# Convolution taps by what GpSimd does, a new order of the begin, and the logarithm's table loaded at other places

## The chip, the cores and the metric

The kernel runs on one core of one Trainium2 chip. The metric is the device time of one execution in microseconds (us), the lower the better. Engines are named as the profile names them: PE (TensorE matmul) with PEld (its weight load), DVE (VectorE), ACT (ScalarE), POOL (GpSimd), SP (SyncE, which issues most DMAs).

## The reference

Two blocks of two layers each over 256 tokens of 1024 features, float32. The first block carries two streams, x and a context c, each 256 tokens. Only the first block is touched by most of the change:

```python
for l in range(2):
    sh1, sc1, g1, sh2, sc2, g2 = adaln(c, w_mod[l], b_mod[l])   # silu(c) @ w_mod, both streams
    h  = modulate(rms_norm(x,  norm1_g[l]), sh1, sc1)
    hc = modulate(rms_norm(xc, norm1_g[l]), csh1, csc1)
    # q, k (rms-normed, rotated), v, pool input, conv inputs a and b
    q, k, v, up, ca, cb = project_inputs(h, w_in[l], q_norm_g[l], k_norm_g[l])
    ...                                    # the same for hc
    attn   = diff_attn_post(diff_attention(q, k_all, v_all, lam), ...)
    pool_o = pool_mixer(up, ...)           # moving means of 2, 4, 8, 16 tokens
    conv_o = silu(layer_norm(depthwise_conv31(ca * sigmoid(cb))))
    x = x + g1 * (concat(attn, pool_o, conv_o) @ w_out[l])
    x = x + g2 * swiglu(modulate(rms_norm(x, norm2_g[l]), sh2, sc2), ...)
    ...                                    # xc likewise, in layer 0 only
```

The second block has, per layer, two kinds of attention and a gated feed-forward with a 3-tap convolution (gate is silu); of it the change touches only where ACT loads a table.

## The kernel before

All activations lie feature-major in SBUF. Weights come from HBM in pieces of 128 x 2048 floats (1 MB) into three raw buffers (`raw`, slot = piece number mod 3), issued by SP. A weight piece of a projection is split for PE: ACT copies it to a rounded part `wh` (step `split`), then DVE makes the rest `wl` = raw - wh. Activations are split the same way (`hx_hi`, `hx_lo` and so on). A product is three matmuls: hi by wh (L1329), hi by wl (L1332), lo by wh (L1334). Pieces of `w_mod` are used raw, by 4 small matmuls each (step `mod`); eight of them make a third of a layer's modulation, which ACT copies out (`modc`) and PE and DVE finish (`modend`).

Nothing is scheduled by the hardware: `plan_program` writes one list of steps, and each engine walks that list and performs its own part of each step, in this order and with waits on semaphores. A step that waits holds back all that stands behind it on its engine. `Plan.take` hands out the next weight piece; its `look` emits the splits and DMAs that buffers allow (`Plan.look`: at most 3 split pieces are held, and a `mod` piece keeps its raw buffer until its matmuls are done).

The begin: squares of c (`nsq`, ACT; POOL adds them), four `mod` pieces, the root of c's norm (`nroot`: PE sums over features with a matrix of ones, ACT does Ln and Exp), four more `mod` pieces, `modend`, c's normalised activation (`nfin`: DVE multiplies, ACT adds the shift and rounds, DVE makes the lo part, eight chunks of 256), squares of x, the gemm of part b for c, and only then (`start_x`) the root and `nfin` of x, the lambdas of the attention, and the gemm of part b for x.

`inproj1` runs over the parts b, a, p, q0, k0, v0, q1, k1, v1 and, in each, over the streams (layer 0: c and x; layer 1: x, with a second generator for c's k and v). Part a fills a list `bg` with the 31 taps x 2 halves of the depthwise convolution of its stream, each one DVE instruction (`tap`, L1741, a scalar_tensor_tensor of 128x256); `pump(n)` emits n of them. Part p starts the moving means on POOL (`pool`, 15 instructions a stream, L2015 to L2026). From q1 on, the attention of the same layer is woven between the projections (`weave`; `scores`, `exps`, `weights`, `turned`, `values`).

After c's attention: `conv_post` (its first part takes the mean, `two` the variance, Ln, Exp, scaling and silu) for c, `pc_split` of c, the same for x, then the output projection of c woven with the attention of x and the modulation pieces of layer 1.

ACT holds one table set at a time. Silu and sigmoid need others than Ln and Exp; `fn` (L1514 to L1525) calls `preload_act_table_set` (L1518) before an Ln or Exp when another set was last used, and stands behind the wait of that step. The loads of the other sets appear at L1523.

## Time and profile before

| | |
|---|---|
| time before, median of 3 runs | 1796.46 us (1794.7 to 1797.76) |
| the profiled execution's own time | 1794.97 us |
| its span, first to last instruction | 1793.1 us |
| mean granted TensorE clock | 0.977 of full |
| PE busy | 94% of the span |
| DVE, ACT, POOL busy | 59%, 49%, 11% |

The profile is one execution. A timeline row is: start in us from the span's start, duration in us, engine, line, operation, output and inputs by the program's names, shape, how many merged, and in brackets how long the engine had been idle and what ended that. In the windows, PEclk is the granted clock as a share of full speed (1.00 is 2.4 GHz, 0.50 is 1.2 GHz).

### The profile page before, as it was taken

What the parts mean: (1) busy time and instruction counts of PE and PEld (TensorE: products, weight loads), DVE (VectorE), ACT (ScalarE), POOL (GpSimd) and SP (SyncE); (2) the same over time, 40 slices, a digit from 0 to 9 for tenths busy, and PEclk for the clock granted to TensorE, in tenths of its full rate; (3) what the DMA queues carried; (4) which work ended last, traced back from release to release, by engine and by line L of the source; (5) the groups of instructions that cost most, each with busy time, mean ns of one, the idle gap of its engine ahead of it and who ended that gap; (6) DMA issues with size and microseconds to landing.
All of it is one profiled execution on the core that took longest, in us unless ns stands there. A gap on an engine that the chain in (4) does not pass through costs nothing. (4 is left out here: it accounts for less than half of the span.)

```text
span 1793.1 us, 30262 instructions
## 1 busy us (share of the span) xinstructions
PE 1685.8 (94%) x12864; PEld 1526.0 (85%) x12864; DVE 1063.0 (59%) x1472; ACT 886.3 (49%) x1192; POOL 192.7 (11%) x138
## 2 busy tenths in 40 slices
PE   5899988999999999997999999988999999889999
PEld 2777666999999999965899989757999987679999
DVE  2498657644445444986644445755776456657773
ACT  3334555544345434555544335655555366556552
POOL 1140000122003210300022100000011000000110
PEclk7899999999999999999999999999999999999999
DMA  9233646466446545363266453302555533025553
GB/s 368 94 141 136 240 165 216 184 235 252 171 165 211 185 174 182 141 238 138 99 221 201 172 174 130 132 22 86 186 184 194 177 120 134 24 95 184 184 195 119
DMA packets 45110, 299.12 MB, mean 167 GB/s; under 512 B 5216, under 2 KB 7360, under 8 KB 11696
## 3 DMA queue, kind: packets, MB, share of 16 engines
q1 hardware_dynamic: 44304, 295.65, 46.0%
q8 instruction: 102, 1.67, 0.4%
q0 software_dynamic: 240, 0.79, 0.1%
q10 hardware_dynamic: 432, 0.75, 0.1%
q14 instruction: 32, 0.26, 0.0%
HBM read 296.10 MB, written 1.06 MB: 166 GB/s over the span
## 5 line engine op out<-in xcount | busy, mean ns | idle before, releaser
L1749 DVE TENSOR_TENSOR wl<-raw,wh 128x2048 fp32r<-128x2048 f32 (+3 forms) x236 | 529.0, 2242 | 520.8 <-ACT wh L1523 470.0
L1523 ACT ACTIVATE wh<-raw 128x2048 fp32r<-128x2048 f32 (+3 forms) x236 | 436.8, 1854 | 259.4 <-PE bank L1334 158.8
L1329 PE MATMUL bank<-hx_hi,wh 128*128 128x256 f32 x1920 | 547.9, 285 | 16.3 <-ACT hx_hi L1523 9.7
L1332 PE MATMUL bank<-hx_hi,wl 128*128 128x256 f32 x1920 | 539.8, 281 | 3.3 <-DVE wl L1749 3.3
L1334 PE MATMUL bank<-hx_lo,wh 128*128 128x256 f32 x1920 | 540.4, 281 | 0.0
L1329 PEld LDWEIGHTS bank<-hx_hi,wh 128*128 128x128 f32 x1920 | 364.0, 190 | 23.9 <-issue 19.7
L1332 PEld LDWEIGHTS bank<-hx_hi,wl 128*128 128x128 f32 x1920 | 364.3, 190 | 8.8 <-DVE wl L1749 4.6
L1334 PEld LDWEIGHTS bank<-hx_lo,wh 128*128 128x128 f32 x1920 | 363.8, 189 | 0.5 <-DVE hx_lo L1741 0.2
L1332 PE MATMUL bank<-hid_hi,wl 128*128 128x256 f32 x880 | 245.4, 279 | 0.5 <-DVE wl L1749 0.5
L1334 PE MATMUL bank<-hid_lo,wh 128*128 128x256 f32 x880 | 245.4, 279 | 0.0
L1329 PE MATMUL bank<-hid_hi,wh 128*128 128x256 f32 x880 | 245.3, 279 | 0.0
L1329 PE MATMUL bank<-hc_hi,wh 128*128 128x256 f32 x752 | 218.8, 291 | 6.2 <-issue 2.7
L1332 PE MATMUL bank<-hc_hi,wl 128*128 128x256 f32 x752 | 215.2, 286 | 7.6 <-DVE wl L1749 7.6
L1334 PE MATMUL bank<-hc_lo,wh 128*128 128x256 f32 x752 | 214.6, 285 | 1.3 <-DVE hc_lo L1856 0.8
L1332 PEld LDWEIGHTS bank<-hid_hi,wl 128*128 128x128 f32 x880 | 165.2, 188 | 0.8 <-DVE wl L1749 0.8
L1334 PEld LDWEIGHTS bank<-hid_lo,wh 128*128 128x128 f32 x880 | 165.1, 188 | 0.0
L1329 PEld LDWEIGHTS bank<-hid_hi,wh 128*128 128x128 f32 x880 | 165.0, 187 | 0.0
L1329 PEld LDWEIGHTS bank<-hc_hi,wh 128*128 128x128 f32 x752 | 146.1, 194 | 19.5 <-issue 19.2
L1332 PEld LDWEIGHTS bank<-hc_hi,wl 128*128 128x128 f32 x752 | 146.1, 194 | 9.0 <-DVE wl L1749 8.6
L1334 PEld LDWEIGHTS bank<-hc_lo,wh 128*128 128x128 f32 x752 | 146.2, 194 | 2.0 <-DVE hc_lo L1856 0.9
L1523 ACT ACTIVATE tmp<-bank,vec 128x256 f32<-128x256 f32 (+3 forms) x188 | 105.8, 586 | 70.1 <-PE bank L1334 39.7
L2031 POOL TENSOR_TENSOR hid_lo<-tmp,hid_hi 128x512 fp32r<-128x512 f32 x33 | 91.7, 2779 | 349.7 <-ACT hid_hi L1523 349.7
(208 smaller groups left out, 1955.0 us busy)
## 6 DMA issues: line engine op xcount, KB each, us to landing
raw<-in_wts SPq DMA_DIRECT2D x258, 1024.0 KB, 4.8
raw<-in_wts SPq DMA_DIRECT2D x20, 768.0 KB, 4.0
raw<-in_wts SPq DMA_DIRECT2D x4, 576.0 KB, 3.5
tmp<-tscr SPq DMA_DIRECT2D x16, 128.0 KB, 4.3
raw<-in_wts SPq DMA_DIRECT2D x2, 640.0 KB, 3.9
xTc<-in_ctxT SPq DMA_DIRECT2D x1, 1024.0 KB, 10.8
xTx<-in_xT SPq DMA_DIRECT2D x1, 1024.0 KB, 8.6
out_x<-xTx POOLq DMA_DIRECT2D x3, 256.0 KB, 5.5
```

The lines of the kernel that those rows point to most:

```text
L1329: pe.matmul(out, hi[:, k, c:c + m], x_hi, start=first and k == 0 and o == 0, stop=False, skip_group_check=True)
L1332: pe.matmul(out, lo[:, k, c:c + m], x_hi, start=False, stop=False, skip_group_check=True)
L1334: ins = pe.matmul(out, hi[:, k, c:c + m], x_lo, start=False, stop=last and k == nk - 1, skip_group_check=True)
L1523: return act.activation(out, in_, func, bias=bias, scale=scale)
L1749: tt(M.wl[k][:, 0:ne], M.raw[f["r"]][:, 0:ne], M.wh[k][:, 0:ne].bitcast(F32), ALU.subtract).then_inc(*on.inc(f["tlo"]))
L2031: tt(lo, y.t[:, :], hi.bitcast(F32), ALU.subtract).then_inc(*on.inc(t[1]))
```

## The change

It does six things. (1) In the first eight `mod` pieces `look` is made only up to the fourth, so that the split of the first projection weight comes behind `modc` and `modend`. (2) At the begin the squares of x are emitted ahead of c's `nfin`, and x's root and `nfin` directly behind c's, ahead of the first gemm; only the lambdas stay between the first two gemms. (3) `inproj1` emits 4 taps a step while POOL computes means (part p, and q0 of the first stream), 10 in the others, instead of 9. (4) `conv_post` becomes three parts; in layer 0 the Ln and Exp of c and x come together, then the silus of both, ahead of c's `pc_split`, and the round of the weave that stood idle goes away. (5) In `attention1` the first `exps` comes ahead of the first yield. (6) A step `log_set` loads the table of Ln and Exp: at the begin, behind each sigmoid, behind the silus of the convolution, behind the last silu of each feed-forward, and behind the first silu where a norm is due in the second round.

```diff
--- before.py
+++ after.py
@@ -448,7 +448,7 @@
     mod_bank, t_mod, mod_late = {}, {}, []
 
     def mod_piece(l, cb, k):
-        f = take(("mod", l, cb, k), look=k < 7)
+        f = take(("mod", l, cb, k), look=k < (4 if (l, cb) == (0, 0) else 7))
         if k == 0:
             mod_bank[0] = banks.get()
         b = mod_bank[0]
@@ -543,9 +543,10 @@
                 mul = p.gemm_tok if part[0] == "v" else p.gemm_pair
                 bank, tk = mul(f, H[s], toks[s], done=s == streams[-1])
                 hfree[s] = [tk]
+                pooling = part == "p" or part == "q0" and s == streams[0]
                 pump(2)
                 run_pending()
-                pump(7)
+                pump(2 if pooling else 8)
                 project1(l, s, part, bank, tk)
                 yield
             if pool_at:
@@ -561,6 +562,7 @@
             t_sg = ev("sig")
             sig_of[s] = (sg, t_sg)
             step("sig", b=b, tk=tk, sg=sg, free=sg.free, t=t_sg)
+            step("log_set")
             banks.give(b, t_sg)
         elif part == "a":
             sg, t_sg = sig_of[s]
@@ -628,13 +630,18 @@
 
         def two():
             v, rs = banks.get(), tmps.get()
-            t2, t_ln, t_rs, t_n, t_x = ev("mm"), ev("ln"), ev("rs"), ev("cdev"), [ev("cact"), ev("cact")]
-            step("conv2", l=l, s=s, v=v, v_free=v.free, sq=sq, a=a, rs=rs, rs_free=rs.free, t=t2, t_ln=t_ln,
-                 t_rs=t_rs, t_n=t_n, t_x=t_x)
+            t2, t_ln, t_rs, t_n = ev("mm"), ev("ln"), ev("rs"), ev("cdev")
+            step("conv2", s=s, v=v, v_free=v.free, sq=sq, a=a, rs=rs, rs_free=rs.free, t=t2, t_ln=t_ln,
+                 t_rs=t_rs, t_n=t_n)
             tmps.give(sq, t2)
             banks.give(v, t_ln)
             tmps.give(rs, t_n)
-            conv_tok[s] = [t_x[1]]
+
+            def three():
+                t_x = [ev("cact"), ev("cact")]
+                step("conv3", l=l, s=s, t_n=t_n, t_x=t_x)
+                conv_tok[s] = [t_x[1]]
+            return three
         return two
 
     mix_of = {}
@@ -707,8 +714,8 @@
             return norm
 
         scores(0)
+        exps(0)
         yield
-        exps(0)
         scores(1)
         norms = []
         for u in range(8):
@@ -792,6 +799,8 @@
         region_free[:] = [tk]
         return nrm, t
 
+    behind = []
+
     def ffn1(l, s, toks, fill=None):
         hid_toks, late = [], []
         for i in range(11):
@@ -803,6 +812,8 @@
             sl = tmps.get()
             a = ev("silu")
             step("silu", b=bg_, tk=tg, sl=sl, free=sl.free, t=a)
+            if i == 10 or i == 0 and behind:
+                step("log_set")
             banks.give(bg_, a)
             bu, tu = p.gemm_pair(("up1", l, 2 * i + 1), H[s], toks)
             y = tmps.get()
@@ -878,16 +889,12 @@
     n["c"].root()
     mod_fill(4, (0, 1, 0))
     mod_flush()
-    toks["c"] = finish0("c")
     p.look()
     for pr in range(4):
         n["x"].add(pr, t_x["x"])
-
-    def start_x():
-        n["x"].root()
-        toks["x"] = finish0("x")
-        lambdas()
-    before_x.append(start_x)
+    for s in "cx":
+        toks[s] = finish0(s)
+    before_x.append(lambdas)
     gi = inproj1(0, "cx", toks, ["b", "a", "p", "q0", "k0", "v0", "q1", "k1", "v1"])
     for i in range(13):
         next(gi)
@@ -898,11 +905,14 @@
     finish_conv(0, "x")
     p.look()
     stage_split("c", "c")
-    two.pop(0)()
+    for three in [fn() for fn in two]:
+        three()
+    step("log_set")
     pc_split("c", "c")
     idle = lambda: None
-    weave(chain(steps(lambda: two.pop(0)()), attention1(0, "x", "x")),
-          chain(steps(idle), outproj1(0, "c", "c", BY_COLS, norm)),
+    two.clear()
+    weave(attention1(0, "x", "x"),
+          outproj1(0, "c", "c", BY_COLS, norm),
           mod_steps(1, (1, 1, 3)),
           steps(idle, idle, idle, lambda: pc_split("x", "x")))
 
@@ -916,7 +926,7 @@
     next(ox)
     finish_ffn_in("c")
     weave(ox)
-    behind = [lambda: finish_ffn_in("x")]
+    behind.append(lambda: finish_ffn_in("x"))
 
     def ffn_step(i):
         mod_fill(i % 2, (1, 2, 0))
@@ -945,7 +955,11 @@
         finish_conv(1, "x")
 
     keys, proj, piece = (lambda: next(gc)), (lambda: next(gx)), (lambda: next(out))
-    norm_half, mix_half = (lambda: two.pop(0)()), (lambda: pc_split("x", "c"))
+    def norm_half():
+        two.pop(0)()()
+        step("log_set")
+
+    mix_half = lambda: pc_split("x", "c")
     fill = ((keys, proj), (proj, keys), (proj, conv_half), (norm_half, mix_half), (piece,), (piece,))
     for fns in fill:
         for fn in fns:
@@ -1278,6 +1292,8 @@
                 (yg, tg), (yu, tu) = res
                 sg, m, t = ev("silu"), ev("gate"), (ev("hid_hi"), ev("hid_lo"))
                 step("gate2", i=i, yg=yg, tg=tg, yu=yu, tu=tu, sg=sg, m=m, free=rf, t=t)
+                if i == 10:
+                    step("log_set")
                 tmps.give(yg, m)
                 tmps.give(yu, *t)
                 hid_toks.extend([t, t])
@@ -1512,11 +1528,14 @@
     eps = M.vcol("eps")
     table = [None]
 
+    def log_set():
+        if table[0] != LOG_SET:
+            act.preload_act_table_set(LOG_SET)
+        table[0] = LOG_SET
+
     def fn(out, in_, func, scale=1.0, bias=0.0, accum=None):
         if func in (ACT.Ln, ACT.Exp):
-            if table[0] != LOG_SET:
-                act.preload_act_table_set(LOG_SET)
-            table[0] = LOG_SET
+            log_set()
         elif func not in (ACT.Copy, ACT.Identity, ACT.Square):
             table[0] = func
         if accum is None:
@@ -1535,6 +1554,7 @@
         act.dma_start(M.vec[:, :], io["vecs"]).then_inc(*on.inc(t_vec, 16))
         on.wait_ge(t_c, z)
         fn(M.csil[:, :, 0:2], M.craw[:, :, :], ACT.Silu).then_inc(*on.inc(t_cs))
+        log_set()
         on.wait_ge(t_vec)
 
     def split(f, free):
@@ -1596,9 +1616,11 @@
         on.wait_ge(t_d, sq_free)
         fn(sq.t[:, :], M.pc[s][:, 2:4, :].rearrange("p a t -> p (a t)"), ACT.Square).then_inc(*on.inc(a))
 
-    def conv2(l, s, v, rs, rs_free, t, t_ln, t_rs, t_n, t_x, **_):
+    def conv2(v, rs, rs_free, t, t_ln, t_rs, **_):
         on.wait_ge(t, rs_free)
         rsqrt(rs, v.t[:, 0:T], T, 1.0 / 256, t_ln, t_rs)
+
+    def conv3(l, s, t_n, t_x):
         on.wait_ge(t_n)
         for j in range(2):
             y = M.pc[s][:, 2 + j, :]
...
```

## Rows read from the trace of the kernel before

**Rows 1.** The page of the kernel before, part 1: busy time, share of the span, instructions.
```profile
PE 1685.8 (94%) x12864; PEld 1526.0 (85%) x12864; DVE 1063.0 (59%) x1472; ACT 886.3 (49%) x1192; POOL 192.7 (11%) x138
```
**Rows 2.** Waits of PE: line, who ended the wait, us in total, times, longest.
```profile
PE bank L1332 <- DVE wl L1749: 11.4, 10, 3.7
```
**Rows 3.** Timeline of PE, 9 to 67 us: start, us, operation, [idle before <-releaser].
```profile
29.17 1.94 PE L1354 MATMUL bank<-raw,csil 128*32 128x512 f32 x8 [3.29 <-DMA raw<-in_wts]
34.05 1.12 PE L1379 MATMUL bank<-cst,tmp 128*128 128x128 f32 x4 [2.94 <-ACT tmp L1523]
...
49.48 4.11 PE L1354 MATMUL bank<-tmp,cst 128*128 128x256 f32 x10 [3.58 <-POOL tmp L2010]
...
56.95 0.58 PE L1329 MATMUL bank<-hx_hi,wh 128*128 128x256 f32 x1 [3.36 <-ACT hx_hi L1523]
...
65.69 1.06 PE L1354 MATMUL bank<-raw,csil 128*32 128x512 f32 x8
```
**Rows 4.** Timeline of ACT and GpSimd, 31 to 48 us.
```profile
31.60 1.91 ACT L1523 ACTIVATE wh<-raw 128x2048 fp32r<-128x2048 f32 x1 [6.19 <-DMA raw<-in_wts]
...
42.88 1.90 ACT L1523 ACTIVATE wh<-raw 128x2048 fp32r<-128x2048 f32 x1
...
44.69 2.18 ACT L1523 ACTIVATE tmp<-xTx 128x512 f32<-128x512 f32 x4
...
45.38 2.38 POOL L2005 TENSOR_TENSOR tmp<-tmp 128x256 f32<-128x256 f32 x1 [29.59 <-ACT tmp L1523]
```
**Rows 5.** DMA issues, window 31.1 to 31.3 us: count, size, us to landing.
```profile
raw<-in_wts SPq DMA_DIRECT2D x1, 1024.0 KB, 8.4
```
**Rows 6.** Windows: us, then PE, PEld, DVE, ACT, POOL busy, PEclk, DMA share, GB/s.
```profile
56.95:65.70 8.75, 8.75 (x51) 8.59 (x51) 7.11 (x22) 4.89 (x9) 0.00 (x0) 0.64 0.00 0
66.68:72.60 5.92, 5.92 (x54) 5.92 (x51) 0.00 (x0) 1.13 (x1) 0.00 (x0) 1.00 0.79 304
...
109.13:117.30 8.17, 8.17 (x48) 8.17 (x49) 8.17 (x13) 1.92 (x1) 4.28 (x5) 0.67 0.40 136
...
237.14:244.60 7.46, 7.46 (x49) 7.34 (x48) 3.61 (x4) 2.39 (x2) 0.74 (x1) 0.76 0.00 0
...
1074.20:1079.50 5.30, 5.30 (x34) 5.30 (x35) 5.16 (x14) 3.24 (x8) 0.30 (x1) 0.73 0.01 2
```
**Rows 7.** Taps on DVE, 86.3 to 113.9 and 113.9 to 119.6 us: ns min/median/max.
```profile
L1741 DVE SCALAR_TENSOR_TENSOR pcc<-upadc,vec,pcc x23: 855/956/1525, 88.2 to 113.1; 128x256 f32<-128x256 f32 x23
...
L1741 DVE SCALAR_TENSOR_TENSOR pcc<-upadc,vec,pcc x14: 471/473/951, 113.1 to 119.3; 128x256 f32<-128x256 f32 x14
```
**Rows 8.** Timeline of DVE and PE, 105 to 110 us.
```profile
105.92 3.15 DVE L1749 TENSOR_TENSOR wl<-raw,wh 128x2048 fp32r<-128x2048 f32 x1
...
109.13 0.58 PE L1332 MATMUL bank<-hc_hi,wl 128*128 128x256 f32 x1 [3.70 <-DVE wl L1749]
```
**Rows 9.** Timeline of ACT and PE, 213 to 237 us.
```profile
233.01 1.28 ACT L1518 ACT_TABLE_LOAD   x1 [3.89 <-DVE st L1737]
...
219.91 0.39 PE L1334 MATMUL bank<-hc_lo,wh 128*128 128x256 f32 x1 [0.75 <-DVE hc_lo L1856]
...
235.14 2.07 PE L1354 MATMUL bank<-k,q1x 64*128 64x512 f32 x2 [5.11 <-ACT e L1524]
```
**Rows 10.** Timeline of ACT and PE around the norms of the later stages.
```profile
332.20 1.28 ACT L1518 ACT_TABLE_LOAD   x1 [4.15 <-PE bank L1354]
333.49 0.47 ACT L1523 ACTIVATE tmp<-bank,vec 128x256 f32<-128x256 f32 x1
...
345.16 0.39 PE L1332 MATMUL bank<-hc_hi,wl 128*128 128x256 f32 x1 [1.56 <-DVE wl L1749]
...
1074.20 0.55 PE L1329 MATMUL bank<-hx_hi,wh 128*128 128x256 f32 x1 [3.31 <-issue]
...
1243.17 0.35 PE L1329 MATMUL bank<-hx_hi,wh 128*128 128x256 f32 x1 [2.08 <-ACT hx_hi L1523]
```
**Rows 11.** Timeline of DVE in the projections of layer 1, 774 to 792 us.
```profile
781.05 2.28 DVE L1749 TENSOR_TENSOR wl<-raw,wh 128x2048 fp32r<-128x2048 f32 x1
```

More of the change, by code:

```diff
@@ L1725, in scalar_program @@
                 "hn2": hn2, "sig": sig, "pool": pool, "poolproj": poolproj, "vcopy": vcopy, "conv1": conv1,
-                "conv2": conv2, "exp1": exp1, "turn1": turn1, "val1": val1, "sub1": sub1, "pcsplit": pcsplit,
+                "conv2": conv2, "conv3": conv3, "log_set": log_set, "exp1": exp1, "turn1": turn1, "val1": val1,
+                "sub1": sub1, "pcsplit": pcsplit,
                 "stsplit": stsplit, "silu": silu, "hidsplit": hidsplit, "lambdas": lambdas, "tables": tables,
```

## The prediction

> **What bounds the kernel now.** I read the page first: PE is busy for 1685.8 of 1793.1 us [rows 1], so a change that adds no matmul can only win idle time of PE, some 107 us, and time in which PE runs at the lower of its two clock levels. The waits of PE [rows 2] show no large single cause: the costliest is 11.4 us for `wl` from DVE, in 10 waits. So each wait is read in its stage, in the timelines, and for each the question is which engine ended it and what that engine did just before. The clock is read in the windows [rows 6]: 48 matmuls of a first projection take 8.75 us at a granted clock of 0.64 and 5.92 us at 1.00. PE stood idle ahead of the slow one. A wait thus costs its length and up to some 3 us more.
>
> **The begin.** PE waits 2.94 us for `modc`, then for c's activation, multiplies for c, waits 3.58 us for POOL's sums of x, takes 4.11 us for the root, waits 3.36 us for `hx_hi` and multiplies for x until 65.7 [rows 3]. New order: the last `mod` matmul ends at 29.17 + 1.94 = 31.1 [rows 3], and `modc` no longer stands behind a split of 1.91 us [rows 4], so `modend` is done some 2 us earlier, at about 34. But ACT and DVE now make two splits ahead of c's `nfin`. The second one's piece is issued at 31.2 and lands 8.4 us later, at 39.6 [rows 5]. ACT's half of it runs to 41.5, the four squares of x (2.18 us [rows 4]) to 43.6, DVE's half (2.3 us) to 43.8. c's `nfin` starts there instead of at 36.5: that is a loss of 7 us for the first gemm. POOL's first sum waits for DVE's split, as it does now (2.38 us [rows 4]), so the sums are ready at about 46.2 and the root runs on PE to 50.4 (4.11). c's eight chunks are out at 51 (0.8 us each, as in the chunks now), x's at about 58.5. PE multiplies for c from 50.4 to 56.2 and for x to 61.9, both at 5.8 us, as its clock is up after the root. The end moves from 65.7 to 61.9: **-3.9 us**. If the clock rises one step later it is -1.5; if POOL and DVE hinder each other less, -5.5. Nothing waits on SP: its order is the same, and the slot of the piece behind is freed by a split that ends when it does now, at 36.
>
> **The pools.** While POOL works, a tap takes 956 ns in the median, after it 473 [rows 7]: the taps advance in step with POOL's instructions. 18 taps stand between one split and the next on DVE; the one at 105.92 takes 3.15 us and PE waits 3.70 us for it [rows 8] and then runs its gemm in 8.17 us at 0.67 instead of 5.92 us at 1.00 [rows 6], and the next one's start still slowly. That is 3.7 + 2.3 + 0.9 = 6.9 us. With 4 + 4 taps ahead of it the split is done at about 98, PE asks at 101. The wait goes whole: **-6.9 us**. The 15 taps come back: 10 a step for nine steps, 4 in a tenth. Two steps then hold 20 taps x 0.4 + a split 2.3 + rotations 3.4 = 13.7 us of DVE against some 14.6 us of PE (two gemms 11.7, a `mod` piece 1.1, norm matmuls 1.9). It fits, with little room; two short waits there (0.9 and 2.0 us now) each get 0.4 us and more: **+1.5**, between 0 and 6.
>
> **The convolution's end and the output projection of c.** Now ACT loads four tables here; `exps` of x's first unit waits behind the last, at 233.01, and PE waits 5.11 us for its banks [rows 9] and then takes 7.46 us for a gemm at 0.76 [rows 6]. New: two loads fewer, and `exps` ahead of the split. Against it: with the idle round gone, the next output piece is number 35 instead of 36, so `p.look()` already splits two pieces ahead of `stage_split`; c's lo part comes 2.3 us later than at 219.91 [rows 9], at 222.2, and so does the first gemm. Then Ln, Exp (2x), two silus each, the table and `pc_split` end at 227.4 on ACT and 228.6 on DVE; the maxima end at 230, the exponentials at 231.5. The first gemm ends at about 230 with a slow start, then a `mod` piece, scores, and the second gemm starts at 233.2 instead of 237.14, one `mod` piece (1.1 us) behind, and at full clock (1.5 us): 3.9 - 1.1 + 1.6, **-4.5 us**. Bounds: -6.5, and +1.5 if the late first gemm is all that stays.
>
> **The tables at the norms.** Where a root comes after silus, Ln stands behind a load of 1.28 us [rows 10]. Beside a gemm the root delays DVE's split, and PE waits for it: 1.56 us at 345 [rows 10], and likewise 1.58 at 540 and 0.70 at 725. The load goes to an idle moment of ACT, the waits shrink by at most 1.28: -1.3 - 1.3 - 0.7 = **-3.3 us** (0 if the split behind the new load becomes as late). In two places nothing covers it: PE waits 3.31 us at 1074 (and at 1438), but 2.08 us at 1243, where the same norm has no load [rows 10]. Twice 1.23: **-2.5 us**. After 3.31 us both run at a lower clock first (0.73 for 5.3 us at 1074 [rows 6]); I take that this goes in one of the two, **-1.5** (0 to -3.1). The extra silu and log loads of the feed-forwards stand in ACT's idle time (49% busy) and cost nothing while splits are a gemm ahead.
>
> A rule is weighed here. The row of the load has 1.28 us, from the end of PE's matmul on [rows 10]. The Trainium skill (ScalarE: Activation LUTs, section What ACT_TABLE_LOAD costs) says that every switch costs the load and a drain, 2.66 us in all. By it the two uncovered norms would win 5.3 us instead of 2.5, and the sum would be 2.8 us lower. The difference of the waits, 3.31 - 2.08 = 1.23, disagrees: it is the load alone.
>
> **Layer 1.** Its pool has no wait of PE now. Fewer taps are done there by the next splits' time, good for 2.4 us of DVE. But `exps` of the first unit now stands on ACT ahead of the Exp of q1's norm and of a split: ACT has to wait for DVE's maxima at about 778.8, its exponentials end at 780.4, the split's ACT half at 783.6 and DVE's at 785.9, where it now ends at 783.33 [rows 11] and PE asks for it then. 0 to 2.7, I take **+1.3**. The log load behind the silus delays the first output piece's split by its 1.28 us: **+1.3**.
>
> **Sum**, against the profiled execution's 1794.97: -3.9 - 6.9 + 1.5 - 4.5 - 3.3 - 2.5 - 1.5 + 1.3 + 1.3 = -18.5, so 1776.5. The median of the runs is 1.5 above that execution, so **1778.0**.
>
> **The rivals.**
> - The begin of x's attention gains nothing (+4.5) and the late first gemm costs 2: 1784.5. For it: two splits ahead of `stage_split`. Against: the bank wait of 5.11 us is ended by an exponential that surely comes earlier. 0.14.
> - DVE is the bound once 10 taps stand in a step: the 5.4 us of the pools are lost and the 2.7 of layer 1 paid in full: about 1785. For it: 13.7 of 14.6 us. Against: DVE idles some 2 us before nearly each split now. 0.11.
> - The change doesn't do what it says with the tables: loads come back for the next function on ACT's way, no norm gains (+7.3): 1785.3. 0.05.
> - The low-clock stretches vanish nearly all, which the shorter waits allow: 8 us more, 1770. 0.06.
> - Slower: the exponentials that stand ahead of the splits in both layers. A late split frees its raw buffer late, so the next piece lands late too. If each of the 10 projection steps that are left beside an attention loses the 2.7 us of above, it costs 27 - 1.3 us: 1803.7. It decides from 1.85 us a step. For it: ACT's queue is strict and the piece's slot is tied to it. Against: in layer 0 DVE is not awaited there, and landings lead by more than a gemm. 0.05.
> - Forecast, 0.59, its own range 1771 to 1784.
>
> **How the numbers follow.** 1778 is the forecast's. The range holds 8 in 10: from 1769 (part of the fast clock case) to 1788 (rivals at 1785 with their spread). 0.2% (3.6 us) is about what a measurement can tell from no change. Slower by more has the slower rival's 0.05 and 0.01 of others' tails, 0.06; within it lie 0.03, the far tails of the two rivals at 1785; faster by more: 0.91.
>
> **What would show it.** PE's last matmul of the first x gemm at about 62; no wait for `wl` near 101 to 107 and 0.5 us taps only few while POOL runs; the second output gemm of c at full clock, 12 us or more earlier in the span; PE's waits of 3.31 us at 2.1; 26 table loads instead of 25, none of L1518 with idle PE behind it. Wrong would be: a wait of several us for `wl` or for `tap` after the pools, or c's first gemm past 52 with x's not right behind.

## The result

| | before | after |
|---|---|---|
| median | 1797.76 us (1794.7 to 1800.54) | 1788.25 us (1787.42 to 1791.48) |
| the profiled execution | 1794.97 | 1789.45 |
| its span | 1793.1 | 1787.7 |
| mean granted clock | 0.977 | 0.978 |

The ratio of the medians is 0.9949, 95% interval 0.9936 to 0.9962: 9.5 us faster where 18.5 had been forecast. The median lies 10.3 us above the predicted 1778.0 and a quarter of a us above the range's upper end. Of these 10.3 us, 1.3 is the base (1797.76 where the forecast had 1796.46 for the kernel before) and 9.0 the change. PE's busy time is 3.1 us less than before [rows 1] with the same number of matmuls, and the others are within 2.3 us, so only idle and low-clock time of PE has moved. Page of the changed kernel, part 1:

```profile
PE 1682.7 (94%) x12864; PEld 1524.4 (85%) x12864; DVE 1061.4 (59%) x1472; ACT 888.6 (50%) x1193; POOL 192.4 (11%) x138
```

The way to read such a pair is to take marks that both traces have (the same matmul) and to write down how much earlier each comes. Beside it stands what the forecast's terms add up to there. The last column has the same shift in a second pair of profiles, one more of each kernel, taken later (see "What one profile is worth"):

| mark on PE | before | after | shift | forecast | shift, second pair |
|---|---|---|---|---|---|
| modulation piece behind the first x gemm | 65.69 | 62.30 | -3.4 | -3.9 | -2.9 |
| `modT` matmuls, beside c's attention | 180.71 | 171.41 | -9.3 | -9.3 | -8.0 |
| norm of the convolution (`conv2`) | 213.91 | 211.93 | **-2.0** | -9.3 | -3.9 |
| last three gemms of x's output projection | 299.66 | 295.12 | -4.5 | -13.8 | -9.9 |
| first gemms of layer 1 | 717.95 | 710.21 | -7.7 | -16.4 | -11.0 |
| x's output projection in layer 1 | 870.90 | 864.86 | -6.0 | -14.5 | -7.4 |
| norm at 1074 | 1074.20 | 1066.85 | -7.4 | -15.7 | -9.6 |
| last feed-forward | 1606.73 | 1595.77 | -11.0 | -18.5 | -13.4 |
| end | 1793.1 | 1787.7 | **-5.4** | -18.5 | -13.4 |

In the first pair two places hold the difference to the forecast: 7.3 us lost between 171 and 212 us, and 5.6 us in the last feed-forward. In the second pair the first place is there again, with 4.1 us, and the last is not. The rows of each follow.

**Begin and pools.** Timeline of the changed kernel, PE from 29 to 63 us, DVE and PE from 93 to 102 (start, us, operation, idle before and who ended it):

```profile
31.43 1.12 PE L1395 MATMUL bank<-cst,tmp 128*128 128x128 f32 x4 [0.70 <-ACT tmp L1542]
46.70 4.37 PE L1370 MATMUL bank<-tmp,cst 128*128 128x256 f32 x10 [14.16 <-POOL tmp L2033]
62.30 1.07 PE L1370 MATMUL bank<-raw,csil 128*32 128x512 f32 x8
...
94.77 2.73 DVE L1772 TENSOR_TENSOR wl<-raw,wh 128x2048 fp32r<-128x2048 f32 x1 [2.22 <-ACT wh L1542]
101.46 0.28 PE L1348 MATMUL bank<-hc_hi,wl 128*128 128x256 f32 x1
```

The root waits for POOL until 46.70 (46.2 was expected), x's gemm ends at about 62.4 (61.9). DVE's split ends at 97.5 (98), PE asks at 101.46 and does not wait: the 3.70 us of [rows 8] are gone.

**The 7.3 us.** Timeline of ACT and PE of the changed kernel, 202 to 205 us:

```profile
202.59 1.91 ACT L1542 ACTIVATE wh<-raw 128x2048 fp32r<-128x2048 f32 x1 [4.32 <-DMA raw<-in_wts]
204.40 0.37 ACT L1542 ACTIVATE aT<-bank 128x256 f32<-128x256 f32 x1
204.91 2.05 PE L1370 MATMUL bank<-aT,v 128*128 128x256 f32 x4 [4.59 <-ACT aT L1542]
```

Its DMA issues in the window 195.1 to 195.2 us (count, size, us from issue to landing):

```profile
raw<-in_wts SPq DMA_DIRECT2D x1, 1024.0 KB, 7.4
```

ACT stands still for 4.32 us in front of a split whose piece, issued at 195.1, lands 7.4 us later. Behind the split stands the copy `aT`, ready for ACT since PE's transposition of 198.7, and PE has nothing else to do until it comes. After that wait PE runs at its lower level: the four matmuls of `aT` take 2.05 us where the kernel before has 1.13. In the kernel before this split comes after the attention.

**Output projection of c.** Windows as in [rows 6], of the changed kernel:

```profile
205.00:228.00 23.00, 19.89 (x88) 15.49 (x88) 11.61 (x18) 14.24 (x23) 0.00 (x0) 0.72 0.20 75
229.85:235.78 5.93, 5.93 (x54) 5.79 (x56) 3.15 (x7) 3.37 (x5) 0.00 (x0) 1.00 0.79 330
```

The stage itself won: the second output gemm takes 5.93 us at 1.00 where it took 7.46 at 0.76, and starts 7.3 us earlier (the prediction's sign was 12 or more) though the stage began only 2.0 earlier. But the first window stands at 0.72; in the kernel before the 23.1 us from 213.9 on have 0.86.

**End of x's attention.** The same pattern once more, ACT and PE, 281 to 285 us:

```profile
281.47 1.91 ACT L1542 ACTIVATE wh<-raw 128x2048 fp32r<-128x2048 f32 x1 [4.09 <-DMA raw<-in_wts]
283.28 0.37 ACT L1542 ACTIVATE tmp<-bank 128x256 f32<-128x256 f32 x1
283.70 1.22 PE L1370 MATMUL bank<-tmp,cst 128*128 128x256 f32 x2 [3.05 <-ACT tmp L1542]
```

**Tables.** PE at the places of [rows 10], and behind it ACT's groups of table loads (L1533: the logarithm's set, L1542: the others; count, us busy and mean ns, idle ahead of them):

```profile
338.72 0.39 PE L1348 MATMUL bank<-hc_hi,wl 128*128 128x256 f32 x1 [0.28 <-DVE wl L1772]
532.36 0.38 PE L1348 MATMUL bank<-hx_hi,wl 128*128 128x256 f32 x1 [0.29 <-DVE wl L1772]
1066.85 0.35 PE L1345 MATMUL bank<-hx_hi,wh 128*128 128x256 f32 x1 [2.03 <-issue]
1427.72 0.35 PE L1345 MATMUL bank<-hx_hi,wh 128*128 128x256 f32 x1 [2.03 <-issue]
```

```profile
L1542 ACT ACT_TABLE_LOAD x13 | 16.7, 1283 | 2.4 <-POOL upadc L2020 2.2
L1533 ACT ACT_TABLE_LOAD x13 | 16.7, 1283 | 0.2
```

1.56, 1.58, 3.31 and 3.31 us of waits became 0.28, 0.29, 2.03 and 2.03: each lost 1.28, the load. 26 loads, as expected, and those of the logarithm's set stood with 41.4 us of idle ACT before them and now with 0.2.

**Layer 1.** ACT and PE, 772 to 776 us, and PE at the first output gemm:

```profile
772.74 1.89 ACT L1542 ACTIVATE wh<-raw 128x2048 fp32r<-128x2048 f32 x1
774.54 0.58 ACT L1542 ACTIVATE tmp<-bank 128x512 f32<-128x512 f32 x1
775.17 0.70 PE L1370 MATMUL bank<-tmp,cst 128*128 128x512 f32 x1 [2.38 <-ACT tmp L1542]
...
805.10 0.55 PE L1345 MATMUL bank<-hc_hi,wh 128*128 128x256 f32 x1 [4.13 <-issue]
```

**The 5.6 us at the end.** Both kernels keep PE busy without a gap here, at a granted clock of 1.00. A window of 40 us in the last feed-forward of the kernel before:

```profile
1640.00:1680.00 40.00, 40.00 (x355) 40.00 (x355) 30.44 (x39) 25.62 (x31) 4.77 (x4) 1.00 0.50 171
```

The same window of the changed kernel:

```profile
1640.00:1680.00 40.00, 40.00 (x342) 40.00 (x341) 29.34 (x37) 25.16 (x29) 5.22 (x4) 1.00 0.51 182
```

And PE's timeline in the kernel before where its stream changes its pace:

```profile
1611.33 0.28 PE L1329 MATMUL bank<-hx_hi,wh 128*128 128x256 f32 x1
1611.45 0.28 PE L1332 MATMUL bank<-hx_hi,wl 128*128 128x256 f32 x1
1611.57 0.31 PE L1334 MATMUL bank<-hx_lo,wh 128*128 128x256 f32 x1
1611.72 0.28 PE L1329 MATMUL bank<-hx_hi,wh 128*128 128x256 f32 x1
1611.83 0.28 PE L1332 MATMUL bank<-hx_hi,wl 128*128 128x256 f32 x1
```

355 matmuls against 342 in the same 40 us. The same instructions start either 118 ns apart or 113 (exact start to start; the rows round to 0.12 and 0.11). With one matmul of 0.31 instead of 0.28 us at 1611.6 the one gave way to the other, and the new pace held for 77 us. Of the last feed-forward's 1584 matmuls 1110 ran at 113 in the profile of before, none in that of after: 1110 x 4.5 ns = 5.0 of the 5.6 us. So the profile from which the forecast counted was a lucky one there, and this may be why its 1794.97 stands 2.8 us under the median of 1797.76.

### The profile page after: what moved, and what is told of

Same layout as the page of the kernel before. It is cut to its first block and busy times, and to the rows that moved or that the text cites. A ratio compares the mean times of both kernels' runs of the same rounds, so it can differ in the third digit from the quotient of the medians.

```text
span 1787.7 us, 30261 instructions
## 1 busy us (share of the span) xinstructions
PE 1682.7 (94%) x12864; PEld 1524.4 (85%) x12864; DVE 1061.4 (59%) x1472; ACT 888.6 (50%) x1193; POOL 192.4 (11%) x138
## 5 line engine op out<-in xcount | busy, mean ns | idle before, releaser
L1542 ACT ACTIVATE wh<-raw 128x2048 fp32r<-128x2048 f32 (+3 forms) x236 | 437.1, 1855 | 252.7 <-PE bank L1350 158.0
L1542 ACT ACTIVATE tmp<-bank,vec 128x256 f32<-128x256 f32 (+3 forms) x188 | 105.7, 586 | 105.5 <-PE bank L1350 56.6
L1370 PE MATMUL bank<-tmp,cst 128*128 128x256 f32 (+3 forms) x294 | 113.2, 509 | 27.9 <-POOL tmp L2033 14.2
## 6 DMA issues: line engine op xcount, KB each, us to landing
xTc<-in_ctxT SPq DMA_DIRECT2D x1, 1024.0 KB, 10.7
```

The lines of the kernel that those rows point to most:

```text
L1370: return pe.matmul(out, lhsT, rhs, start=start, stop=stop, skip_group_check=True)
L1542: return act.activation(out, in_, func, bias=bias, scale=scale)
```

## The experiments

All times are medians; those of the kernel before on the same chip lay between 1797.4 and 1799.2 us. A gain in us is worked out from the ratio to them. By their 95% intervals these gains are uncertain by 2 to 4 us.

**One part alone.** Three kernels that add one part each to the kernel before. The taps:

```diff
+                pooling = part == "p" or part == "q0" and s == streams[0]
                 pump(2)
                 run_pending()
-                pump(7)
+                pump(2 if pooling else 8)
```

> The kernel before with only the taps changed (4 a step while GpSimd works, 10 in the others). The forecast's terms: -6.9 for the wait of 3.70 us near 109 and its low clock, +1.5 for the steps with 10 taps: -5.4, 1792.4 us where the kernel before has 1797.8. From the trace of the changed kernel (shift of 6.8 us over the pools, none given back up to 196 us): 1791. Rival (DVE is the bound with 10 taps a step): no gain left, 1796 to 1798, with new waits of PE for wl between 120 and 200 us.

1792.68 us, ratio 0.9958 (0.9943 to 0.9973): 7.6 us faster. The wait near 109 is gone, and PE has no wait for `wl` between 120 and 200 us: the rival falls. Both the forecast's -5.4 and a gain of 6.9 with nothing given back lie inside the interval.

The order of the begin (parts 1 and 2 of the change, as in the diff ahead):

> The kernel before with only the new order of the begin. The changed kernel's first x gemm ended 3.4 us earlier (62.4 instead of 65.8). Theory: that carries through to the end, 1794.4 us against 1797.8. Rival (the shift is absorbed at the wait for wl near 109 us, whose chain hangs on the taps and GpSimd and not on the gemms): PE's wait there grows from 3.7 to about 7 us and the total stays within 1 us of 1797.8.

1796.22 us, ratio 0.9984 (0.9969 to 1.0000): 2.9 us faster, a gain at the edge of what can be told. The row of PE at the taps' split, with the old taps:

```profile
105.30 0.58 PE L1328 MATMUL bank<-hc_hi,wl 128*128 128x256 f32 x1 [3.80 <-DVE wl L1745]
```

It waits 3.80 us, not 7, and stands 43.5 us behind the modulation piece that follows the first x gemm, as it did before (43.4): the chain of POOL and its taps moved along with the gemms. The rival falls. But its 3.8 us against [rows 8] are not all a gain of the edit: in the profiles of e4 and e5 below, which have the old begin, the same matmul comes at 106.40 and 106.20. The modulation piece behind the first x gemm starts at 62.59 to 65.69 us in the five profiles with the old begin (mean 64.2) and at 60.00 to 62.31 in the nine with the new one (mean 61.7): 2.5 us, near the 2.9 of the medians.

The tables (part 6 alone, with the step behind each `conv2`):

```diff
             step("sig", b=b, tk=tk, sg=sg, free=sg.free, t=t_sg)
+            step("log_set")
...
+            if i == 10 or i == 0 and behind:
+                step("log_set")
```

> The kernel before with only the loads of the logarithm's table at the new places. The forecast: -3.3 beside gemms, -2.5 at the two uncovered norms, -1.5 of low clock, +1.3 ahead of layer 1's first output split: -6.0, 1791.8 us against 1797.8. Rival (in the changed kernel the layer's shift between 307 and 1595 us comes from the long runs of matmuls that go at 113 or at 118 ns each, and not from the tables): 1795 or more, with the waits shorter all the same.

1791.67 us, ratio 0.9953 (0.9935 to 0.9972): 8.5 us faster, more than the forecast's 6.0, which lies inside the interval. The rival's 1795 does not.

**The part that lost.** The kernel before with parts 4 and 5, the convolution's end without the idle round and the exponentials ahead of the yield:

```diff
-    two.pop(0)()
+    for three in [fn() for fn in two]:
+        three()
     pc_split("c", "c")
...
-    weave(chain(steps(lambda: two.pop(0)()), attention1(0, "x", "x")),
-          chain(steps(idle), outproj1(0, "c", "c", BY_COLS, norm)),
+    weave(attention1(0, "x", "x"),
+          outproj1(0, "c", "c", BY_COLS, norm),
...
         scores(0)
+        exps(0)
         yield
-        exps(0)
```

> The kernel before with only the third part of the convolution's end, without the idle round, and with the first exponentials ahead of the first yield in both layers; no taps, begin or tables. The forecast had -4.5 and +1.3 for this: 3.2 us faster than before. Theory now: it also moves the first output piece one place up in the order of pieces, so that its split waits on ACT for its landing ahead of c's last attention steps (about +7), wins some 7 at the output projection, loses 3 to 4 at the end of x's attention and 2 to 4 in layer 1: 0 to 5 us slower than before. Rival (the early split hurts only because PE comes earlier in the full change): no wait of PE for aT over 2 us near 213 us, and 3 us faster than before.

1803.63 us against 1797.52, ratio 1.0027 (1.0014 to 1.0041): about 5 us **slower** (2.5 to 7.4). ACT and PE at c's last attention steps, and PE in layer 1:

```profile
207.37 1.91 ACT L1530 ACTIVATE wh<-raw 128x2048 fp32r<-128x2048 f32 x1 [3.74 <-DMA raw<-in_wts]
209.69 0.77 PE L1361 MATMUL bank<-aT,v 128*128 128x256 f32 x1 [4.67 <-ACT aT L1530]
...
783.29 1.22 PE L1361 MATMUL bank<-tmp,cst 128*128 128x512 f32 x1 [3.25 <-ACT tmp L1530]
```

The early split makes its wait without the earlier PE of the full change, so the rival falls. Layer 1 from its first gemms to its output projection takes 138.9 us here, 134.4 and 134.6 in two profiles of the kernel before. By the marks, against the mean of those two profiles, this kernel loses 5.2 us from `modT` to `conv2`, wins 5.4 from there to the last gemms of x's output projection, and loses 4.4 in layer 1.

**The split moved back.** The changed kernel with one look fewer:

```diff
-        f = take(("mod", l, cb, k), look=k < (4 if (l, cb) == (0, 0) else 7))
+        f = take(("mod", l, cb, k), look=k < (4 if (l, cb) == (0, 0) else 6 if (l, cb) == (0, 2) else 7))
```

> The changed kernel with one edit: the look at the seventh modulation piece of layer 0's last third is left out, so that the first split of an output weight comes behind c's attention instead of ahead of its last two steps. In the changed kernel this split stands on ACT at 202.59 us after 4.32 us of waiting for its piece, the last copy of the transposed scores stands behind it, and PE idles 4.59 us at 204.91 and runs at its lower clock after that. Theory (the early split is what cost the missing 7.5 us of the forecast): c's attention ends about 7 us earlier, the two splits then stand ahead of c's lo part and take some 2 to 4 us of that back; about 1783 us (1781 to 1785) where the changed kernel has 1788.3. Rival (the pieces land late anyway and whoever waits first only passes the wait on): the first output gemm of c still starts near 218 us, under 2 us gained, 1786.5 to 1788.5.

ACT and PE of this kernel, 199 to 214 us:

```profile
199.03 0.38 ACT L1542 ACTIVATE aT<-bank 128x256 f32<-128x256 f32 x1 [0.44 <-PE bank L1433]
205.82 1.89 ACT L1542 ACTIVATE wh<-raw 128x2048 fp32r<-128x2048 f32 x1
208.10 1.91 ACT L1542 ACTIVATE wh<-raw 128x2048 fp32r<-128x2048 f32 x1 [0.39 <-DMA raw<-in_wts]
213.59 0.58 PE L1350 MATMUL bank<-hc_lo,wh 128*128 128x256 f32 x1 [2.07 <-DVE hc_lo L1879]
```

`aT` comes at 199.03 instead of 204.40, PE does not wait for it, `conv2`'s norm stands at 205.29 (211.93 in the changed kernel), the first output gemm gets its lo part at 213.59 instead of 218.56, and by 289 us the kernel is 6.1 us ahead (2.5 ahead of a second profile of the changed kernel, below, whose lo part still comes only at 216.62). That is the theory's mechanism, and the rival's 218 is off. The size is less sure. In total it has 1787.09 us, in the rival's range, and ratio 0.9924 (0.9903 to 0.9945) against 0.9949: some 4.5 us of gain, with the intervals overlapping. That is about the mean of 6.1 and 2.5 us, the leads over the two profiles of the changed kernel. Layer 1 took 139.1 us here and 136.1 and 138.0 in those two.

**Layer 1's exponentials.** The changed kernel with the old order in layer 1:

```diff
         scores(0)
-        exps(0)
+        if l == 0:
+            exps(0)
         yield
+        if l == 1:
+            exps(0)
```

> The changed kernel with one edit: in layer 1 the first exponentials stand behind the yield again, as before. Theory: PE's wait of 2.38 us at 775.17 (for tmp from ACT, whose queue holds the exponentials of the first unit ahead) goes, with up to 1.5 us of low clock behind it: 2.4 to 3.9 us faster than the changed kernel, up to layer 1's first output gemm. Rival (the wait is DVE's, which comes late from the maxima and 10 taps a step): PE waits as long there for DVE's wl, and nothing is gained.

1786.67 us, ratio 0.9931 (0.9911 to 0.9951), 3 us ahead of the changed kernel's ratio, with the intervals overlapping. In the profile the wait of 2.38 us is gone and no wait for `wl` takes its place, so the rival falls; the first output gemm of layer 1 starts at 802.76 instead of 805.10. What comes behind it took that back in this execution. The window from there to the next mark in the changed kernel:

```profile
805.10:846.27 41.17, 32.65 (x176) 25.07 (x177) 28.50 (x54) 21.92 (x44) 0.00 (x0) 0.92 0.28 103
```

And in this one:

```profile
802.76:846.20 43.44, 36.39 (x177) 27.90 (x177) 28.50 (x54) 21.89 (x44) 0.00 (x0) 0.82 0.27 97
```

The same work on DVE and ACT, but a granted clock of 0.82 instead of 0.92, and 2.3 us more. This is not the edit's doing alone: the second profile of the changed kernel has 0.86 and 43.26 us in this window.

**A modulation piece first.** The changed kernel with one line, which gives the pieces their order of before and so takes away both late splits:

```diff
     two.clear()
+    mod_fill(1, (1, 1, 3))
     weave(attention1(0, "x", "x"),
```

> The changed kernel with one line: a modulation piece of layer 1 ahead of the weave of x's attention with c's output projection, which gives the pieces their old order (modulation piece 33, output piece 34). No split then stands ahead of c's last attention steps, only one ahead of c's lo part, and each modulation piece of the stage comes one round earlier. Theory: the gain of e1 (6.0 us by 289 us), 2 us more at the lo part, and 2 to 4 us more at the end of x's attention, since the first output piece of x waits there for a raw buffer that a modulation piece frees: 8 to 11 us by 300 us, 1778 to 1781 us where the changed kernel has 1788.3. Rival (x's end hangs on the transfers as such): 6 us by 300 us, with ACT waiting over 3 us for a landing ahead of x's last copy: 1782 to 1783.

1783.92 us, ratio 0.9913 (0.9895 to 0.9931), some 6.5 us ahead of the changed kernel. PE from 211 to 226 us:

```profile
211.38 0.49 PE L1351 MATMUL bank<-hc_lo,wh 128*128 128x256 f32 x1 [0.75 <-DVE hc_lo L1880]
222.94 0.39 PE L1346 MATMUL bank<-hc_hi,wh 128*128 128x256 f32 x1 [1.34 <-ACT wh L1543]
225.33 0.58 PE L1349 MATMUL bank<-hc_hi,wl 128*128 128x256 f32 x1 [2.01 <-DVE wl L1773]
```

By 288 us it is 7.1 us ahead of the first profile of the changed kernel, between theory (8 to 11) and rival (6), and 3.5 of the second; the median is above the range of either. At x's end ACT waits 1.64 us for a landing instead of 4.09 (3.45 in the second profile), so the rival's mechanism is not there. A loss that the theory had not counted stands in the last two rows: the second output piece's split now stands behind the exponentials, and PE waits 3.35 us for it.

**All of it.** The same with layer 1's exponentials behind the yield and without this line:

```diff
     def norm_half():
         two.pop(0)()()
-        step("log_set")
```

> The changed kernel with the modulation piece first, layer 1's first exponentials behind the yield, and no table load ahead of layer 1's first output split. By the terms: -8 to -11 of the first, -2.4 to -3.9 of the second, -1.3 of the third: 1773 to 1776 us where the changed kernel has 1788.3. Rival (layer 1's waits replace one another): no more than the modulation piece gives alone, 1779.

1781.70 us, ratio 0.9902 (0.9885 to 0.9918). The gain is smaller than the theory's (1773 to 1776): the waits of e7 at 222.94 and 225.33 had not been counted. It is 2.2 us below e7 with overlapping intervals, so the medians do not exclude the rival; in the profiles layer 1 up to its output projection takes 135.2 us here and 139.3 in e7. Once more, beside the changed kernel on one chip:

> The kernel of e8 once more, unchanged, beside the changed kernel on one chip. Theory: 8 to 11 us by 300 us and 3.7 in layer 1, of which the lower clock behind the remaining waits takes some back: 6 to 10 us faster than the changed kernel. Rival (half of e8's distance was the chip or the luck of the clock): under 4 us.

1782.75 us, ratio 0.9919 (0.9901 to 0.9936), and the changed kernel 1788.42: 5.7 us, at the lower edge of the theory's 6 to 10.

**Layer 0's exponentials as well.**

```diff
         scores(0)
-        if l == 0:
-            exps(0)
         yield
-        if l == 1:
-            exps(0)
+        exps(0)
```

> The kernel of e8 with the first exponentials behind the yield in layer 0 as well, so that the split of the second output piece stands ahead of them on ACT and DVE. In e8 PE waits 1.34 us for wh at 220.70 and 2.01 for wl at 223.09 and runs the second output gemm of c in 9.7 us with these waits. Theory (the order of this split and the exponentials only decides which of the two is late): both waits go, the exponentials end about 3 us later and PE waits 2 to 3 us for their banks instead: within 1.5 us of e8 by 240 us, in total 1780 to 1783 where e8 had 1781.7. The forecast's step (exponentials first is what wins at x's attention): the wait of 5.11 us of the kernel before comes back, 3 to 5 us slower than e8.

PE and ACT of this kernel, 214 to 222 us:

```profile
214.00 1.90 ACT L1542 ACTIVATE wh<-raw 128x2048 fp32r<-128x2048 f32 x1
219.82 0.69 ACT L1543 ACTIVATE e<-bank,st 128x512 f32<-128x512 f32 x1 [3.91 <-DVE st L1760]
220.65 1.12 PE L1370 MATMUL bank<-k,q1x 64*128 64x512 f32 x2 [1.49 <-ACT e L1543]
221.70 0.39 PE L1345 MATMUL bank<-hc_hi,wh 128*128 128x256 f32 x1
```

1777.76 us, ratio 0.9893 (0.9876 to 0.9910), beside 1782.75 and 1788.42 on the same chip. Both expectations missed: the split goes into a gap that ACT had anyway while it waited for DVE's maxima (3.22 us in e8), PE waits 1.49 us for a bank instead of 3.35 for the weight, and the next gemm runs in 5.92 us at full clock, where that of e8 takes 9.72 us from its first matmul to its last, its wait included. It ends 2.8 us earlier than in e8, 0.7 of which this profile was ahead already at `conv2`. This kernel is the fastest of all, 10.7 us under the changed one.

**What one profile is worth.** The two kernels unchanged:

> The changed kernel once more, unchanged. In the profiles so far its matmuls of 256 columns run in long stretches at either 113 or 118 ns each: in the last feed-forward of the kernel before 1110 of 1584 at 113, in the same stretch of the changed kernel none, 5.6 us longer. Theory (which of the two holds is not set by the change): another profile of the same kernel shows other stretches and another granted clock near 810 to 845 us, so one profile differs from the next by up to 5 us; median again 1788 to 1790. Rival (the change sets it): the same stretches and the same lengths within 0.3 us.

> The kernel before once more, unchanged. The profile on which the forecast rested spends 183.15 us in the last feed-forward of layer 1 (121.90 + 61.25); ten profiles of ten kernels that have the same instructions there spend 187.3 to 188.7. Theory (that one execution was lucky in this stretch, at 113 ns instead of 118 for most matmuls): 187 to 189 us here too, and a profiled execution nearer to the median of 1797.5. Rival (the kernel before has this stretch at its faster pace always, and the change lost it): 183.2 again within 0.5 us.

The changed kernel: 1788.42 us, ratio 0.9952 (0.9937 to 0.9968). Its second profile stands at 291.52 us where the first stood at 295.12 (begin of the last three gemms of x's output projection), spends 138.0 us in layer 1's attention stage instead of 136.1, and 188.68 us in the last feed-forward, as the first did (188.67). So stretches before it do vary by some 2 to 4 us, but this one is the same, and on it the rival was right for the changed kernel. The kernel before: 1798.32 us, ratio 0.9995 (0.9984 to 1.0006), the profiled execution 1803.21. Windows of its last feed-forward:

```profile
1609.54:1735.86 126.32, 126.32 (x1058) 126.22 (x1059) 95.29 (x129) 75.30 (x92) 12.94 (x10) 0.99 0.50 174
1735.70:1798.05 62.35, 62.35 (x530) 62.14 (x528) 27.52 (x22) 19.93 (x15) 3.33 (x5) 1.00 0.39 136
```

188.67 us, not the 183.15 of the first profile. The 13 other profiles all have 187.3 to 188.7. The change didn't lose these 5.6 us; they were never a property of the kernel before. Since the medians do not rest on that execution, these 5.6 us are no part of the 9.0 us that the change fell short.

A stage is judged more safely from all 14 profiles. From the `modT` matmuls to `conv2` the four kernels' profiles with the early split (both of the changed kernel, e5, e6) take 39.1 to 40.7 us, the ten others 33.2 to 35.1: the early split costs 6.2 us in the mean, and the two groups do not overlap. From layer 1's first gemms to its output projection the five profiles with the exponentials ahead of the yield take 136.1 to 139.3 us (mean 138.3), the nine others 133.2 to 137.9 (mean 135.4): 2.9 us, with some overlap.

## Why the prediction was wrong

Step by step, as it was put:

- **Begin, -3.9**: right in kind and somewhat too large. -3.4 in the trace, 2.9 alone (0 to 5.6), 2.5 in the means of the profiles. POOL's sums, the root and both gemms came within 0.7 us of their forecast times.
- **Pools, -6.9, given back +1.5**: right. The split ends at 97.5 us, the wait is gone, the shift at 171.41 us is the forecast's -9.3 (-8.0 in the second pair). The waits for `k` and `modT` grew from 0.88 and 1.97 to 1.50 and 2.37: 1.0 given back. DVE was not the bound: PE's 11.4 us of waits for `wl` [rows 2] are 2.7 now.
- **Convolution's end, -4.5**: **the step that failed**. The sentence was: "with the idle round gone, the next output piece is number 35 instead of 36, so `p.look()` already splits two pieces ahead of `stage_split`". The numbers were right and so was the count of two splits. The place of the first was taken from the kernel before and not followed through the planner: it is not at that `p.look()`, but at the look of modulation piece 31, whose predecessor has just freed the raw buffer of piece 33. There it stands ahead of two attention steps that had no split in front of them, and waits for a landing. In the kernel before piece 34 is the output piece, its buffer comes free one modulation piece later, and that one (k = 7) has no look. e1 shows it: with the split moved the 4.59 us are gone. The bound of +1.5 was too tight, since it knew only a late gemm: e5 has +4.9 for parts 4 and 5. The forecast gave parts 4 and 5 together -3.2 us; the difference to e5, 8.1 us, is nearly the whole of the 9.0 us that the change fell short. What the term was about did come: from `conv2` to the last gemms of x's output projection the two profiles of the changed kernel take 82.1 us in the mean and the two of the kernel before 86.4, 4.3 us less where 4.5 were forecast. The early split took it back ahead of that stretch: from `modT` to `conv2` 39.8 against 34.1. (That term's sum, 3.9 - 1.1 + 1.6, also gives 4.4 and not 4.5.) The total came out 3 to 4 us above the rivals at 1785, by a mechanism that none of them had.
- **Exponentials first**: the prediction said of the 5.11 us wait that it "is ended by an exponential that surely comes earlier". It came earlier, but the order against the split was not what gained. In the kernel before it stood at the end of a chain on ACT and DVE: table loads at 218.11, 222.69 and 224.93 with the halves of the convolution between them, the split at 227.23, DVE's half of it and the maxima to 232.7, and the load at 233.01. In e10, with the convolution's end merged but the exponentials behind the split again, PE waits 1.49 us for them, not 5.11 (6.6 in four other profiles without the change to the convolution's end), and the kernel is 5.0 us faster than with the exponentials ahead (r_best on the same chip). No run takes the loads and the halves apart. In layer 1 the term was +1.3, with PE expected late for `wl` at 783; it is late for `tmp` of the k norm, at 775, by 2.38 us, since the copy stands behind exponentials and split on ACT. The means over the profiles have +2.9 for it. The slower rival was right that ACT's order would make this late; its repetition in ten steps, 27 us, did not come.
- **End of x's attention**: had no term. The attention came earlier, but the output piece it needs waits for the raw buffer of a modulation piece, and the lost idle round had put those one round later. e7 agrees with that: 1.64 us of ACT's wait instead of 4.09, and of PE's behind it 1.81 instead of 3.05; but PE waits 1.82 us there in the first profile of the kernel before and 0.47 in the second, so the size of this is uncertain.
- **Tables, -3.3, -2.5, -1.5**: right, 8.5 alone against 6.0. The low clock did go in one of the two places: the 34 matmuls behind the wait take 4.42 us instead of 5.85 at 1428, and 5.83 instead of 5.38 at 1067; the second profile of the changed kernel has it the other way round, 5.41 and 4.41. The rule weighed (the Trainium skill, ScalarE: Activation LUTs, section What ACT_TABLE_LOAD costs, with 2.66 us a switch) would have left a wait of 0.65 us at 1066.85; the row has 2.03, which is 3.31 less the load of 1.28. A switch between two activations shows no drain either. ACT of the kernel before:

```profile
224.50 0.42 ACT L1523 ACTIVATE tmp<-tmp 128x256 f32<-128x256 f32 x1
224.93 1.28 ACT L1523 ACT_TABLE_LOAD   x1
226.23 1.10 ACT L1523 ACTIVATE pcx<-pcx,vec 128x256 f32<-128x256 f32 x2
```

- **Layer 1's log load, +1.3**: right, 2.71 became 4.13 us.
- **The base**: the sum was made against one execution whose last feed-forward was 5.5 us faster than in the second profile and 4.1 faster than in any other. The step to the median (+1.5, later +2.8) covers such luck; in the medians the base was off by 1.3 us.

The parts alone add up to -7.6 - 2.9 - 8.5 + 4.9 = -14.1 us, the whole has -8.9 (mean of its two ratios). Each of the four is uncertain by 2.4 to 3.3 us, so that the sum is uncertain by nearly 6; whether the parts hinder each other is not settled. If the lost part had given the -3.2 us of the forecast in place of +4.9, the whole would by this count have come to about -17.

## What to carry to other kernels

On an engine that works through its list in order, a step that waits for a transfer is harmless only at the places where the list has nothing urgent behind it. When an edit removes or adds one step of such a plan, write the new list out to the next point where old and new agree and look at where each waiting step has moved, not only at how many there are: one idle round fewer moved one split ahead of the end of an attention, and that cost nearly as much as the pools had given. And take the time of a long stretch from several profiles: two executions of one program can differ in a stretch by more than the edit is worth.

## What the runs showed of the hardware

- Matmuls of 256 columns without a gap start 113 or 118 ns apart, at a granted clock of 1.00 both times. In the profile of before the pace changed at a hiccup of 0.03 us in the stream and again at a wait of 0.55 us, and one pace held for up to 77 us. A feed-forward's 1056 matmuls took 121.90, 124.92 or 126.32 us, the last two in two profiles of the same kernel (r_best and e8). What sets the pace was not tried.
- Behind the wait ahead of layer 1's first output gemm the granted clock of the next 41 to 45 us was 0.92, 0.82, 0.85 and 0.81 in four kernels with nearly the same work there (changed, e6, e8, e7); between the first two that is worth 2.3 us. One kernel differs from itself as much: the changed one had 0.92 in one profile and 0.86 in the other, 41.17 and 43.26 us. The length of the wait does not order them: it was 4.13 us in all of these but e8, which had 2.71. A wait taken away in the stage ahead can be lost again by this in one execution and not in the next.
- A table load of ACT between two activations cost its own 1.28 us and no more (224.93 us in the kernel before).
